# Two RMS norms behind a feed-forward joined to one root, in a one-core Trainium2 kernel

## What is computed

```python
def rms_norm(x, g):                      # EPS = 1e-6
    y = x * lax.rsqrt(jnp.mean(x * x, axis=-1, keepdims=True) + EPS)
    return y * g
...
x = x_mid + gt_f * sq_relu_mlp(modulate(rms_norm(x_mid, g_ffn[l]), sh_f, sc_f), w_ff1[l], w_ff2[l])
x = rms_norm(x, g_final)                 # end of the first model
h_res = jnp.concatenate([meta, x], axis=1)
h = rms_norm_2(h_res, norm_gain[0])      # start of the second
f_in, q, k, v, gate = jnp.split(h @ w_in[0], splits, axis=-1)
...
h_res = h_res + y @ w_out[0]             # h_res is needed again here
```

## Time and profile before

| | |
|---|---|
| median of 3 runs | 2995.29 us |
| the profiled execution | 2999.37 us |
| its span, first to last instruction | 2997.6 us |
| busy: PE, DVE, ACT, POOL | 2699.0, 1256.5, 943.4, 486.9 us |
| PE's share of the span | 90% |
| mean granted TensorE clock | 0.956 of 2.4 GHz |

### The profile page before, as it was taken

The page is one execution under the profiler, slowest core; times in us unless marked ns, Lnnn a source line. Parts: engine busy times, 40 slices in busy tenths (PEclk is TensorE's granted clock), DMA queues, the critical chain, the costliest instruction groups (busy, mean ns, idle before and its releaser), DMA issues. The chain is left out here.

```text
span 2997.6 us, 35474 instructions
## 1 busy us (share of the span) xinstructions
PE 2699.0 (90%) x14559; PEld 2306.6 (77%) x14559; DVE 1256.5 (42%) x1592; ACT 943.4 (31%) x1506; POOL 486.9 (16%) x299
## 2 busy tenths in 40 slices
PE   4999858899879999999992999989999799998999
PEld 1777646799758888888882999868888798767887
DVE  4743552433453333333337422237743522226652
ACT  3412323344242111112203222236731222226640
POOL 0100110342000000000000000018830100007740
PEclk9999978999989999999995999999999899999999
DMA  5541001000201111111102114133111213232212
GB/s 218 169 141 41 22 8 50 15 1 1 98 28 57 50 43 49 49 49 49 49 29 86 52 47 100 36 96 72 41 79 71 80 40 85 54 91 61 67 71 85
DMA packets 65518, 189.21 MB, mean 63 GB/s; under 512 B 7776, under 2 KB 26592, under 8 KB 64224
## 3 DMA queue, kind: packets, MB, share of 16 engines
q1 hardware_dynamic: 65376, 187.21, 19.9%
HBM read 146.79 MB, written 16.97 MB: 55 GB/s over the span
## 5 line engine op out<-in xcount | busy, mean ns | idle before, releaser
L1576 DVE TENSOR_REDUCE da_negmax<-ps 128x1 f32<-128x1040 f32 x136 | 167.7, 1235 | 26.1 <-PE ps L1430 19.3
L2086 DVE SCALAR_TENSOR_TENSOR res<-ps,gates,res 128x1024 f32<-128x1024 f32 x64 | 79.2, 1279 | 226.1 <-PE ps L2135 226.1
L1561 POOL TENSOR_TENSOR da_E<-da_E,da_F 128x1040 f32<-128x1040 f32 x68 | 163.8, 2409 | 5.7
L1473 PE MATMUL ps<-da_aT,v 128*128 128x128 f32 (+1 forms) x1224 | 159.1, 276 | 0.7 <-ACT qk L1533 0.7
L2135 PE MATMUL ps<-ff_h_lo,ff_wh 128*128 128x512 f32 x512 | 157.8, 389 | 0.0
L2135 PE MATMUL ps<-ff_h_hi,ff_wh 128*128 128x512 f32 x512 | 157.7, 389 | 0.0
L2135 PE MATMUL ps<-ff_h_hi,ff_wl 128*128 128x512 f32 x512 | 157.7, 389 | 0.0
L2049 ACT ACTIVATE ff_wh<-ff_raw 128x1024 fp32r<-128x1024 f32 x64 | 67.6, 1057 | 284.2 <-PE ps L2135 278.3
L1473 PEld LDWEIGHTS ps<-da_aT,v 128*128 128x128 f32 x1224 | 152.0, 196 | 1.1 <-ACT qk L1533 1.1
L2123 PE MATMUL ps<-ffn_in_hi,ff_wh 128*128 128x512 f32 x480 | 149.4, 393 | 2.2 <-DVE ff_wl L2072 2.2
L2123 PE MATMUL ps<-ffn_in_lo,ff_wh 128*128 128x512 f32 x480 | 149.9, 394 | 0.0
(11 more groups left out here) (462 smaller groups left out, 6243.6 us busy)
## 6 DMA issues: line engine op xcount, KB each, us to landing
ff_raw<-w_ff SPq DMA_DIRECT2D x64, 512.0 KB, 3.2
ada_w<-w_ada SPq DMA_DIRECT2D x16, 1024.0 KB, 7.5
wo_raw<-w_out SPq DMA_DIRECT2D x18, 512.0 KB, 5.1
residual_spill<-res SPq DMA_DIRECT2D x2, 4160.0 KB, 11.2
st_q<-st_q_rounded SPq DMA_DIRECT2D x32, 260.0 KB, 5.1
res<-xT SPq DMA_DIRECT2D x2, 4096.0 KB, 14.1
ada_w<-w_ada SPq DMA_DIRECT2D x4, 2048.0 KB, 26.4
pqk_raw<-w_in SPq DMA_DIRECT2D x16, 512.0 KB, 4.1
```

The costliest lines, as they stand in the source:

```text
L1473: mm = pe.matmul(k.ps[:, pv_bank(g), 0:w], v(g // NQ, t), aT[g % 2][:, t, 0:w], start=(t == 0), stop=(t == NT - 1))
L1561: pool.tensor_tensor(e, e, f, ALU.add).then_inc(s_A, 1)
L1576: dve.tensor_reduce(nm[:, n % 4:n % 4 + 1], window(n), AX.X, ALU.max, negate=True).then_inc(s_nm, 1)
L2086: last = dve.scalar_tensor_tensor(out=res[:, m, :], in0=k.ps[:, 4 * s + 2 * t:4 * s + 2 * t + 2, :].rearrange("p c w -> p (c w)"), scalar= ...
```

## The change

`final_norm` and its phase are gone. `JoinedNorm` computes both norms at once. With S1 the mean of x^2, the second norm of the scaled x is x g_final g_2 / sqrt(mean(x^2 (g_final^2 + EPS)) + EPS^2), so its squares are taken of the unscaled x with the factor sqrt(g_final^2 + EPS) per feature (`join_gains_act`), and both gains are multiplied once (`join_gains_dve`). The meta columns are squared without the factor and get a constant on top.

Squares and additions of tiles 0 to 7 stand in the last four units of the feed-forward, and each tile is squared twice: `square_join` for the joined norm (16 meta columns, then 1024), `square_x` for the first norm alone, whose root still scales the residual. In unit 3 PE posts a second semaphore, `s_half`, behind the first of its two tiles. The feed-forward now also fetches the meta tokens at its start and the projection's first weights behind its last ones, splits them into high and low, and ends with the sums, the roots and the joined reciprocals.

The projection skips the split of its first weights. Its tiles are scaled in two pieces, 16 and 1024 columns. Beside it, `KeepResidual` takes the reciprocals of the first norm's roots, scales the residual in place, and stores it in 8 tiles, for which SP waits before the phase ends.

```diff
-def final_norm(nc, k, norm, follow, load, then):
...
+class JoinedNorm(RmsNorm):
...
+    def join_meta(self, sp):
+        sp.dma_start(*self.meta).then_inc(self.s_meta, 16)
+    def join_fetch(self, sp, w_lo, count, raw):
+        for s in (0, 1):
+            sp.wait_ge(w_lo[s], count)
+            sp.dma_start(raw[:, s, :], self.then(s)).then_inc(self.s_w[s], 16)
...
+    def square_join(self, act, m):
+        act.wait_ge(self.s_x, m + 1)
+        if m == 0:
+            act.wait_ge(self.s_meta, 16)
+            act.wait_ge(self.s_gain, 2)
+        if m >= 2:
+            act.wait_ge(self.s_accj, m - 1)
+        act.activation(self.sq_join[m % 2][:, 0:META], self.k.res[:, m, 0:META], ACT.Square)
+        act.activation(self.sq_join[m % 2][:, META:], self.x(m), ACT.Square, scale=self.root[:, m:m + 1]).then_inc(self.s_sqj, 1)
+    def square_x(self, act, m):
+        if m >= 2:
+            act.wait_ge(self.s_accx, m - 1)
+        act.activation(self.sq_x[m % 2][:], self.x(m), ACT.Square).then_inc(self.s_sqx, 1)
+    def add_join(self, dve, m):
+        acc, sq = self.rstd[0], self.sq_join[m % 2]
+        dve.wait_ge(self.s_sqj, m + 1)
+        if m == 0:
+            dve.tensor_scalar(acc[:, 0:META], sq[:, 0:META], KD * (EPS - EPS * EPS), None, ALU.add)
+            dve.tensor_copy(acc[:, META:], sq[:, META:]).then_inc(self.s_accj, 1)
+        else:
+            dve.wait_ge(self.s_accj, m)
+            dve.tensor_tensor(acc[:], acc[:], sq[:], ALU.add).then_inc(self.s_accj, 1)
+    def add_x(self, dve, m):
+        dve.wait_ge(self.s_sqx, m + 1)
+        if m == 0:
+            dve.tensor_copy(self.rx[:], self.sq_x[0][:]).then_inc(self.s_accx, 1)
+        else:
+            dve.wait_ge(self.s_accx, m)
+            dve.tensor_tensor(self.rx[:], self.rx[:], self.sq_x[m % 2][:], ALU.add).then_inc(self.s_accx, 1)
+    def split_hi(self, act, s, raw, wh):
+        act.wait_ge(self.s_w[s], 16)
+        act.activation(wh[:, s, :], raw[:, s, :], ACT.Copy).then_inc(self.s_whi, 1)
+    def split_lo(self, dve, s, raw, wh, wl):
+        dve.wait_ge(self.s_whi, s + 1)
+        dve.tensor_tensor(wl[:, s, :], raw[:, s, :], wh[:, s, :].bitcast(F32), ALU.subtract).then_inc(self.s_wlo, 1)
+    def join_sums(self, pe):
+        ps = self.k.ps
+        pe.wait_ge(self.s_accj, KD)
+        for c, (a, w) in enumerate(self.parts[0]["chunks"]):
+            pe.matmul(ps[:, c, 0:w], self.k.ones[:], self.rstd[0][:, a:a + w], start=True, stop=True).then_inc(self.s_sum, 1)
+        pe.wait_ge(self.s_accx, KD - 1)
+        pe.wait_ge(self.s_sqx, KD)
+        for c, (a, w) in enumerate(self.cx):
+            pe.matmul(ps[:, 4 + c, 0:w], self.k.ones[:], self.rx[:, a:a + w], start=True, stop=False)
+            pe.matmul(ps[:, 4 + c, 0:w], self.k.ones[:], self.sq_x[(KD - 1) % 2][:, a:a + w], start=False, stop=True).then_inc(self.s_sumx, 1)
+    def join_roots(self, act):
+        k = self.k
+        for c, (a, w) in enumerate(self.parts[0]["chunks"]):
+            act.wait_ge(self.s_sum, c + 1)
+            act.activation(self.rstd[0][:, a:a + w], k.ps[:, c, 0:w], ACT.Sqrt, bias=k.vec[:, V_EPS_SQ:V_EPS_SQ + 1], scale=1.0 / DM)\
+               .then_inc(self.s_root, 1)
+        for c, (a, w) in enumerate(self.cx):
+            act.wait_ge(self.s_sumx, c + 1)
+            act.activation(self.rx[:, a:a + w], k.ps[:, 4 + c, 0:w], ACT.Sqrt, bias=k.vec[:, V_EPS:V_EPS + 1], scale=1.0 / DM)\
+               .then_inc(self.s_rootx, 1)
...
+    def tiles_dve(self, dve):
+        p = self.parts[0]
+        for n in range(self.n + 1):
+            if n < self.n:
+                if n >= 3 and self.by_pool(n - 3):
+                    dve.wait_ge(self.s_plo, self.pool_before(n - 2))
+                elif n >= 3:
+                    dve.wait_ge(self.s_lo, n - 2 - self.pool_before(n - 2))
+                z, r = self.z[n % 3], self.rstd[0]
+                dve.scalar_tensor_tensor(out=z[:, 0:META], in0=self.k.res[:, n, 0:META], scalar=p["gain"](n),
+                                         in1=r[:, 0:META], op0=ALU.mult, op1=ALU.mult)
+                dve.scalar_tensor_tensor(out=z[:, META:L2], in0=self.x(n), scalar=self.both[:, n:n + 1],
+                                         in1=r[:, META:], op0=ALU.mult, op1=ALU.mult).then_inc(self.s_z, 1)
...
+class KeepResidual(Side):
...
+    def dve(self, dve, m):
+        norm = self.norm
+        if m == 0:
+            for a, w in norm.cx:
+                dve.reciprocal(norm.rx[:, a:a + w], norm.rx[:, a:a + w]).then_inc(self.s_r, 1)
+        if m == 2:
+            dve.wait_ge(self.s_r, len(norm.cx))
+            for q in range(KD):
+                dve.scalar_tensor_tensor(out=norm.x(q), in0=norm.x(q), scalar=norm.k.vec[:, V_GFIN + q:V_GFIN + q + 1],
+                                         in1=norm.rx[:], op0=ALU.mult, op1=ALU.mult).then_inc(self.s_scaled, 1)
+    def sp_last(self, sp):
+        for q in range(KD):
+            sp.wait_ge(self.s_scaled, q + 1)
+            sp.dma_start(self.spill[:, q, :], self.norm.k.res[:, q, :]).then_inc(self.s_kept, 16)
+        sp.wait_ge(self.s_kept, 16 * KD)
...
 # gemm, the SP stream
                     fetch_first(sp, k, then)
+                if side:
+                    side.sp_last(sp)
...
 # feed_forward
+        is_end = lambda g, kind: isinstance(g, int) and g == NG - 1 and kind == 2
         is_zero = lambda j: isinstance(j, int) and j == 0
         with nc.Block() as block:
...
                         return
                     sp.wait_ge(w_lo[s], j)
                     sp.dma_start(raw[:, s, :], w[bass.ds(row, P), :]).then_inc(w_in[s], 16)
+                join.join_meta(sp)
                 schedule(sp, unit)
+                join.join_fetch(sp, w_lo, 4 * NG, raw)
             @block.scalar
             def _(act):
...
                 hi(0, 0)
                 hi(1, 0)
                 norm.tiles_act(act)
+                join.join_gains_act(act)
                 def unit(kind, g, par, u, s, j, row, f):
+                    if is_end(g, kind) and u == 3:
+                        join.square_join(act, 6)
+                        join.square_x(act, 6)
+                        join.square_join(act, 7)
+                        act.wait_ge(done[s], j + 1)
+                        join.split_hi(act, 1, raw, wh)
+                        join.square_x(act, 7)
+                        join.join_roots(act)
+                        return
                     act.wait_ge(done[s], j + 1)
+                    if is_end(g, kind):
+                        if u == 2:
+                            join.split_hi(act, 0, raw, wh)
+                        else:
+                            hi(s, j + 1)
+                        for m in (2 * u, 2 * u + 1):
+                            join.square_join(act, m)
+                            join.square_x(act, m)
+                        return
                     if kind == 1:
                         if not is_zero(f):
...
                 lo(0, 0)
                 lo(1, 0)
                 norm.tiles_dve(dve)
+                join.join_gains_dve(dve)
                 def unit(kind, g, par, u, s, j, row, f):
                     if kind == 1:
...
                         dve.sem_inc(freed[s], 1)
                         dve.tensor_tensor(rt[:, s, :], rt[:, s, :], rt[:, s, :], ALU.mult).then_inc(sqd[s], 1)
                     else:
-                        dve.wait_ge(done[s], j + 1)
                         for t in range(2):
                             m = 2 * u + t
+                            if is_end(g, kind) and m == 6:
+                                dve.wait_ge(join.s_half, 1)
+                            else:
+                                dve.wait_ge(done[s], j + 1)
                             last = dve.scalar_tensor_tensor(
                                 out=res[:, m, :], in0=k.ps[:, 4 * s + 2 * t:4 * s + 2 * t + 2, :].rearrange("p c w -> p (c w)"),
                                 scalar=gate[:, m:m + 1], in1=res[:, m, :], op0=ALU.mult, op1=ALU.add)
-                        last.then_inc(freed[s], 1)
+                            if is_end(g, kind):
+                                last.then_inc(join.s_x, 1)
+                            if is_end(g, kind) and m == 6:
+                                join.add_join(dve, 6)
+                                join.add_x(dve, 6)
+                        if not is_end(g, kind):
+                            last.then_inc(freed[s], 1)
+                        elif u < 2:
+                            dve.sem_inc(freed[s], 1)
                     if not is_last(g, kind, u):
                         lo(s, j + 1)
+                    if is_end(g, kind):
+                        for m in ((2 * u, 2 * u + 1) if u < 3 else (7,)):
+                            join.add_join(dve, m)
+                            if m < KD - 1:
+                                join.add_x(dve, m)
+                        if u >= 2:
+                            join.split_lo(dve, u - 2, raw, wh, wl)
```

(37 more changed lines are left out.)

68 lines of the change are left out of this document (29 added, 39 removed).

## The result

The changed kernel takes 2953.2 us (median of four runs, 2951.95 to 2954.89) against 2995.28 (2994.91 to 2996.0): a ratio of 0.9854, 95% interval 0.9843 to 0.9866. The forecast was 2954.3 in a range of 2951.0 to 2959.0. The profiled execution took 2954.89 us with a span of 2953.1, the one of before 2999.37 and 2997.6.

What follows compares the result with a forecast made beforehand. PE is busy 90% of the run, so only its pauses matter; the one between feed-forward and projection waits on DVE. Cutting it from 61.0 to 20.0 us gives 2995.3 - 41.0 = 2954.3 us, range 2951.0 to 2959.0.

Steps and rivals of the forecast that it cites:

- residual 6: Feed-forward tail: DVE adds residual tile 6 at once, the half-way semaphore having come by 1573.1; ends at 1577.3.
- residual 7: Feed-forward tail: DVE adds residual tile 7 behind both additions of tile 6, 1.28 us, ending at 1582.2.
- the first sum: PE's column sums behind the feed-forward can start after tile 7's square and its addition on DVE, at 1584.7.
- the last reciprocal's end: End of the feed-forward phase: last of three reciprocals on DVE, 8.83 us from PE's sums starting, at 1593.6.
- The pause and the saving: Between PE's last feed-forward and first projection matmul: 20.0 us instead of 61.0, so 41.0 us less.
- The phase change: Between the feed-forward's last reciprocal and the projection's first instruction: 0.85 us, ending at 1594.4.
- The small pieces: Meta tokens' 16-column pieces on DVE and ACT: 0.1 us each, with 0 and 0.25 as bounds.
- Rival A: PE stays at 1.2 GHz through the first norm's x sums, giving back 3.3 us: 2957.6; chance 0.12.
- Rival B: Sqrt in the feed-forward brings ACT table loads, 0.4 up to 1.3 us each place: 2955 to 2957; chance 0.04.
- Rival C: DVE's pieces, reciprocals or scalings in the projection make PE wait for a split, 3 us: 2957.3; chance 0.06.
- Rival D: The residual's store in eight pieces outlasts its cover in the projection; at the slow rate about 3099 us; chance 0.02.
- The better end: PE not falling to the lower clock: 0.6 us at the sums, 2.2 at the restart, 2951.5; chance 0.01.

Runs made afterwards that it cites:

- e5: The changed kernel with the four products for the first norm's sums made twice; 2952.85 us, ratio 0.9832–0.9864.
- e2: The changed kernel with the projection's first weights split in the projection again, not beside the feed-forward; 2957.16 us, ratio 0.9845–0.9878.
- e7: The changed kernel with DVE adding residual 7 ahead of tile 6's additions, tile 6's plain squares last; 2952.81 us, ratio 0.9831–0.9864.
- e4: The changed kernel with the eight pieces of the residual stored twice, 8320 KB in all; 2966.89 us, ratio 0.9878–0.9913.
- e8: The changed kernel with useless matmuls (24, 12 and 16) filling PE's waits; 2952.45 us, ratio 0.9829–0.9862.
- e12: e9 with eighteen useless matmuls behind the sums instead of ten; 2947.24 us, ratio 0.9821–0.9852.
- e9: The changed kernel with residual 6 earlier, residual 7 ahead of tile 6's additions and in halves, and 8, 10 and 14 useless matmuls; 2951.18 us.

## Why the prediction was right, step by step

In times behind PE's last matmul (predicted, measured): residual 6 2.50 ahead of it, 2.50; both additions begin at 0.1, 0.10; residual 7 at 2.5, 2.40; its addition at 5.0, 4.99; the first sum at 6.2, 6.29; the last reciprocal's end at 15.1, 15.12; the next phase's first instruction at 15.9, 16.10; PE at 20.0, 20.17. The sum's terms hold within 0.2 us each. The points:

- **The pause and the saving**: 41.0 predicted, 60.98 - 20.17 = 40.8 measured. The medians differ by 42.1. The profiled executions differ by 44.5 in span; the 3.2 beyond the pause and the half (0.5) lie outside this stretch, and no step of the change explains them: 1.1 us ahead of PE's last feed-forward matmul, which stands anywhere from 1573.08 to 1577.58 in traces of the same code (e5, e2), the rest behind the projection. The profiled execution of before was 4.1 above its median and that of the change 1.7, which makes 2.4 of the 3.2; the rest is open. That the forecast came within 1.1 us of the median is in part luck, since the change's own two medians lie 0.9 apart; the pause is what was predicted and hit.
- **The phase change** was mis-sized: 0.98 (1592.53 to 1593.51, and as much in the change again) for 0.85. e2 has 0.97 with ACT first in the next phase, so it is not the engine; where the 0.13 us come from no run shows.
- **The small pieces**: 16 columns on DVE cost 0.15 us each (1593.51 to 1593.66), taken at 0.1 with a bound of 0.25; on ACT 0.12 (1576.22 to 1576.34). The square with a scale per partition took 1.14, taken at 1.15.
- **Rival A** (lower clock through the x sums) did not come: the clock returned between 1587 and 1588 (0.91 granted), 3.6 us behind the first sum. The x sums ended at 1590.85, 13.4 us behind PE's last matmul, where I had 13.9. It was not far off, though: in e2 and e7 the clock came back only in the x sums (the first two took 1.91 and 1.83 us instead of 1.02), and the last x root ended within 0.06 us of the last reciprocal.
- **Rival B** (table loads): none. So the Trainium skill's rule (ScalarE: Activation LUTs, section Table sets: the hidden batching unit) did not bear on it; Square, Sqrt, Copy and Relu ran in the feed-forward without a load.
- **Rival C**: the mechanism was near. The slack ahead of the split was 0.63 and not 1.2 us: eight pieces of 0.15 took 1.2 us instead of 0.5 to 0.7. PE still waited 0.76 us at that place, as before.
- **Rival D**: the stores landed at 1643.3, 3.8 us ahead of the phase's end (2.6 ahead of PE's last matmul); predicted were 5. The first store went out where I had it (1673.1 in old time, predicted 1673); the eight pieces took 12.1 us instead of 11.2, and the phase's end came 0.5 earlier. e4 shows where the loss begins.
- **The better end** that I gave 0.01 was the right size: with PE kept at the upper clock e8 gains 0.4 in the pause (the reciprocals begin 0.7 earlier, the last dummies take 0.3 back) and 1.2 to 2.6 in the half.
- **The step missed** is none of the sum but of the half: I took the clock's return at the projection's start as one number. It varies from one execution to the next (below), by 1.4 us.

## What to carry to other kernels

A chain of norms between two matmul stages is worth looking at as one: what the second needs that the first's squares already know can be joined, and of the 40.8 us gained here 27.4 came from that and only 13.4 from moving the squares and the weights' split under the matmuls. Behind the last matmul the order of the vector engine's queue is the path: work of an earlier tile belongs behind the last tile's first step, and reciprocals that only a later stage needs belong under that stage. Where effects are smaller than the scatter of executions, read the stretch in the trace: the pause repeated here to 0.01 us in four kernels with the same tail, where single executions moved by several.

## What the runs showed of the hardware

Over the eleven traces without dummies (the one of before among them, 25.76) the same projection half took 25.23 to 26.60 us, and the restart makes the difference. In the ten of the changed kernels the half follows the clock granted in the second 3 us behind the restart: 0.98 and 0.96 with 25.23 and 25.28 us, 0.84 with 25.58, 0.66 and 0.63 with 26.08 and 26.19, 0.52 to 0.50 with the five of 26.47 to 26.60. In the first 3 us it was 0.50 in both traces of the change. The second 3 us of the change:

```profile
1600.58:1603.58 3.00, 3.00 (x20) 3.00 (x20) 3.00 (x3) 0.08 (x1) 1.80 (x1) 0.96 0.00 0
```

the change again:

```profile
1598.44:1601.44 3.00, 3.00 (x12) 3.00 (x12) 3.00 (x3) 1.07 (x1) 2.97 (x1) 0.50 0.00 0
```

Idle for 1.56 and 1.59 us (e8, e12), PE was still at 2.4 GHz (granted 1.00); idle for 3.20 us (e9), it was granted 0.86 over the gap and 0.50 behind it, for 6 us of matmuls that followed closely. e9:

```profile
1587.50:1590.60 3.10, 0.00 (x0) 0.00 (x0) 2.12 (x3) 0.00 (x0) 0.32 (x2) 0.86 0.00 0
1590.60:1593.60 3.00, 2.95 (x7) 2.41 (x8) 3.00 (x4) 1.82 (x2) 0.00 (x0) 0.50 0.75 262
```

Eight stores of 520 KB, issued 1.2 us apart, landed 5.0 us after their issue (median) and took 12.1 us together: 4.26 MB at 352 GB/s, where the one store of 4160 KB had 377 (11.3 us).
